# Low parts of the sixth token operand made by GpSimd instead of VectorE at three phase changes

## What is computed

```python
h = rmsnorm(x, norm_g)
proj = jnp.einsum('btd,dc->btc', h, w_in)
xa, za, v, bg, cg, zb, ga, gb = jnp.split(proj, SPLIT_IDX, axis=-1)
ya, new_pool = pool_mixer(xa, pool_buf, offset, w_pool_mix, pool_scale)
ya = ya * jax.nn.silu(za)
yc, new_conv = conv_mixer(cg * v, conv_buf, w_conv)
yb = bg * yc * jax.nn.silu(zb)
merged = (jax.nn.sigmoid(ga + b_gate[:D_MODEL]) * jnp.einsum('bte,ed->btd', ya, w_proj_pool)
          + jax.nn.sigmoid(gb + b_gate[D_MODEL:]) * jnp.einsum('bte,ed->btd', yb, w_proj_conv))
x = x + jnp.einsum('btd,de->bte', merged, w_out)
```

## Time and profile before

| | us |
|---|---|
| median of 3 runs | 2438.61 |
| lowest and highest run | 2438.40 and 2442.47 |
| the profiled execution | 2441.29 |
| its span, first to last instruction | 2439.3 |
| PE busy | 2400.9 (98%) |
| DVE busy | 1681.2 (69%) |
| ACT busy | 891.8 (37%) |
| GpSimd busy | 113.3 (5%) |

### The profile page before, as it was taken

How to read it: one execution, slowest core, us unless ns; L and a number is a source line. 1 busy time by engine, 2 the same in 40 slices (tenths; PEclk the granted TensorE clock), 3 DMA queues, 4 the chain that set the end, 5 groups by cost and what they waited for, 6 DMA issues and landing times.

```text
span 2439.3 us, 42617 instructions
## 1 busy us (share of the span) xinstructions
PE 2400.9 (98%) x17834; PEld 2338.0 (96%) x17834; DVE 1681.2 (69%) x2298; ACT 891.8 (37%) x1306; POOL 113.3 (5%) x216
## 2 busy tenths in 40 slices
PE   7999999999999999999999999999999999999997
PEld 6999999999999999999999999999999999888886
DVE  6556666666666686777868777865755876877666
ACT  7423333333333343323322222233533533432535
POOL 2000000000000000000000000000000011100001
PEclk9999999999999999999999999999999999999999
DMA  6454333333333453434433343245555767998656
GB/s 228 154 202 151 126 108 107 108 108 108 108 108 108 160 206 136 161 135 148 150 131 114 134 139 139 100 178 197 209 164 181 274 241 272 317 338 310 234 210 224
DMA packets 197069, 422.23 MB, mean 173 GB/s; under 512 B 12329, under 2 KB 113757, under 8 KB 182032
## 3 DMA queue, kind: packets, MB, share of 16 engines
q1 hardware_dynamic: 171200, 286.16, 34.6%
q0 software_dynamic: 24224, 127.33, 13.9%
q10 hardware_dynamic: 1456, 6.03, 0.7%
HBM read 283.10 MB, written 135.86 MB: 172 GB/s over the span
## 4 chain that ended last, share of the span: by engine, by line
PE 92%; DMA 3%; DVE 2%; ACT 1%; issue 1%; POOL 0%; ACTq 0%; SPq 0%; DVEq 0%
PE ps L1275 73%; PE ps L1400 10%; PE ps L1317 6%; PE ps L1462 1%; PE ps L1422 1%; DMA rest<-in_x_sample_dram 1%; DVE ops L2060 1%; DMA mt_raw<-opq 1%; DMA xn<-in_x_prompt_dram 1%; DMA tb_in<-opq 0%; DMA ops_raw<-opq 0%; DVE lo L1916 0%; ACT junk L1800 0%; PE ps L1438 0%; DVE pb L2055 0%
## 5 line engine op out<-in xcount | busy, mean ns | idle before, releaser
L1275 PE MATMUL ps<-ops,hi 128*128 128x272 f32 x9888 | 1349.1, 289 | 4.9 <-DVE pb L2055 4.0
L1275 PEld LDWEIGHTS ps<-ops,hi 128*128 128x128 f32 x9888 | 1286.3, 188 | 6.4 <-DVE pb L2055 4.7
L1275 PE MATMUL ps<-ops,lo 128*128 128x272 f32 x4944 | 720.6, 288 | 0.0
L1275 PEld LDWEIGHTS ps<-ops,lo 128*128 128x128 f32 x4944 | 658.4, 188 | 0.0
L1523 ACT ACTIVATE hi<-sb 128x512 fp32r<-128x512 f32 x432 | 273.2, 632 | 576.9 <-PE ps L1275 447.2
L2055 DVE TENSOR_TENSOR pb<-pb,ps 128x544 f32<-128x544 f32 x342 | 246.1, 720 | 268.0 <-PE ps L1275 267.8
L1916 DVE TENSOR_TENSOR lo<-sb,hi 128x512 fp32r<-128x512 f32 x432 | 297.6, 689 | 162.3 <-ACT hi L1523 158.3
L1523 ACT ACTIVATE hi<-raw 128x512 fp32r<-128x512 f32 x268 | 169.4, 632 | 371.2 <-PE ps L1275 358.6
L1916 DVE TENSOR_TENSOR lo<-raw,hi 128x512 fp32r<-128x512 f32 x268 | 184.7, 689 | 116.2 <-ACT hi L1523 116.2
L1400 PE MATMUL ps<-ms_hi,mt 128*128 128x512 f32 x896 | 222.7, 391 | 2.6 <-DVE mt L2298 2.6
L1400 PEld LDWEIGHTS ps<-ms_hi,mt 128*128 128x128 f32 x896 | 168.8, 189 | 38.6 <-DVE mt L2298 3.0
(11 more groups left out here) (158 smaller groups left out, 1510.9 us busy)
## 6 DMA issues: line engine op xcount, KB each, us to landing
raw<-in_w_in_dram SPq DMA_DIRECT2D x158, 512.0 KB, 3.9
pb<-part SPq DMA_DIRECT2D x39, 1088.0 KB, 6.1
part<-pb POOLq DMA_DIRECT2D x37, 1088.0 KB, 5.3
mt_raw<-opq SPq DMA_DIRECT2D x28, 1024.0 KB, 6.0
gates<-pb POOLq DMA_DIRECT2D x16, 1088.0 KB, 9.3
gate<-gates SPq DMA_DIRECT2D x32, 544.0 KB, 6.5
ms<-in_w_out_dram SPq DMA_DIRECT2D x16, 1024.0 KB, 9.8
ops_raw<-opq SPq DMA_DIRECT2D x15, 1088.0 KB, 6.9
```

The lines of the kernel that those rows point to most:

```text
L1275: mm = nc.tensor.matmul(ps[b][:, c, 0:HC], w[:, w_slot, kt * P:(kt + 1) * P], operand[:, kt, half, c * HC:(c + 1) * HC], start=fresh and k ...
```

## The change

GpSimd takes over the low part of operand 5, the sixth, at each of the three phase changes. `operand_lo` of DVE returns at once for it, and GpSimd has a function of its own with the same subtraction on the same tiles. It counts on a semaphore of its own, `pool_lo`, for which PE waits ahead of the second eight matmuls of q = 5. The counts of `ops_lo` become six per phase instead of seven (`lows_of`), at every place that waits for them.

```diff
+    BY_POOL = 5
+
+    def lows_of(ph, o):
+
+        return (NQ - 1) * (ph - 1) + o + (o < BY_POOL)
...
+        pool_lo = sem("pool_lo")
...
-                        sp.wait_ge(ops_lo, operands_of(YA, 6))
+                        sp.wait_ge(ops_lo, lows_of(YA, 6))
...
+            def operand_lo(ph, o):
+
+                pool.wait_ge(ops_hi, operands_of(ph, o))
+                nc.gpsimd.tensor_tensor(ops[:, o, :, 1, :], ops_raw[o][:, :, 1, :], f32(ops[:, o, :, 0, :]),
+                                        ALU.subtract).then_inc(pool_lo, 1)
...
+                if s in SPLIT and SPLIT[s][1] == BY_POOL:
+                    operand_lo(*SPLIT[s])
...
-                    halves = (ops_hi, ops_lo, operands_of(ph, q))
+                    halves = (ops_hi, ops_lo, operands_of(ph, q), lows_of(ph, q))
+                    if q == BY_POOL:
+                        halves = (ops_hi, pool_lo, operands_of(ph, q), ph)
...
             def operand_lo(ph, o):
+                if o == BY_POOL:
+                    return
                 dve.wait_ge(ops_hi, operands_of(ph, o))
```

More of the change, by code:

```diff
@@ L872, in load_operand @@
                     if ph == YB and o == 0:
-                        sp.wait_ge(ops_lo, operands_of(YA, 6))
+                        sp.wait_ge(ops_lo, lows_of(YA, 6))
                     if o == 6:
-                        sp.wait_ge(ops_lo, operands_of(ph, 0))
+                        sp.wait_ge(ops_lo, lows_of(ph, 0))
                     dst = waiting[ph][o][:, :, :]
@@ L1271, in terms @@
                     if w is hi and halves is not None:
-                        pe.wait_ge((halves[0], halves[1])[half], halves[2])
+                        pe.wait_ge(halves[half], halves[2 + half])
                     for kt in range(KQ):
@@ L1292, in first_product @@
                 place, _ = FIRST_OPS[f]
-                terms(i % 2, (SLOT0 + 4 * g + n) % R, ops[:, place], 4 * g + n + 1, (first_hi, first_lo, f + 1),
+                terms(i % 2, (SLOT0 + 4 * g + n) % R, ops[:, place], 4 * g + n + 1, (first_hi, first_lo, f + 1, f + 1),
                       i in (0, 1, 4, 5))
@@ L1360, in product @@
                 if g == NC:
-                    halves = (first_hi, first_lo, (1, 5, 6, 4, 7, 2, 8)[q])
+                    halves = (first_hi, first_lo, *2 * ((1, 5, 6, 4, 7, 2, 8)[q],))
                 elif ph > H0 and j == 0:
-                    halves = (ops_hi, ops_lo, operands_of(ph, q))
+                    halves = (ops_hi, ops_lo, operands_of(ph, q), lows_of(ph, q))
+                    if q == BY_POOL:
+                        halves = (ops_hi, pool_lo, operands_of(ph, q), ph)
                 terms(bank(s), s % R, ops[:, q], split_of_slot(s), halves, q in (0, 1, 5))
@@ L2099, in block_sums @@
                         dve.wait_ge(merged, 2 * ((ph - M0) * KQ + kt) + 2)
-                        dve.wait_ge(ops_lo, operands_of(YB, 6))
+                        dve.wait_ge(ops_lo, lows_of(YB, 6))
                 for k, (d, one, other) in enumerate(((dst[:, 0, :], src[1], src[0]),
@@ L2125, in window @@
                     else:
-                        dve.wait_ge(ops_lo, operands_of(H1, 6))
+                        dve.wait_ge(ops_lo, lows_of(H1, 6))
                 if c == 1 and k == 0:
```

## The result

| kernel | median, us | against before, 95% interval | profiled execution, us | its span, us |
|---|---|---|---|---|
| before | 2438.70 (6 runs) | | 2441.29 | 2439.3 |
| after | 2447.59 (6 runs, 2445.11 to 2448.83) | 1.0032 [1.0022, 1.0042] | 2447.26 | 2445.2 |

The changed kernel is slower: by 8.9 us between the medians, by 7.7 us (0.32%, to which the interval belongs) between the means. The whole interval lies beyond 0.2%. The six times of before form two groups, four at 2438.4 to 2438.8 us and two at 2441.7 and 2442.5 us, so that their median is uncertain by a microsecond; against the 33 further executions of before with which e1 to e4 are compared (median 2439.6) the changed kernel is 8.0 us slower. All executions compared in this document were in the fast state, but for one of e2 (2586.7 us at a granted clock of 0.849), which is left out of its ratio.

The account below looks back on a forecast made before the run. PE was taken to bound the kernel, with waits at three phase changes. From 2438.6 us, 6.8 us of moves and 3.0 of clock, 9.8 together, gave 2448.4 us; range 2434.3 to 2453, the forecast's own 2442.5 to 2453.

Parts of the forecast that it names:

- The bound: Whole kernel: PE, busy 2400.9 of 2439.3 us, bounds it; a microsecond PE stands still is one of the whole.
- What comes off DVE: At the three phase changes: three subtractions of 128x2176 leave DVE, 2.33 us each to the next step's start.
- GpSimd's time: Each moved subtraction on GpSimd, called D: 4.8 us, between 3.84 (two passes) and 5.8 (three passes).
- The mutual block: At the phase changes: while GpSimd reads SBUF, DVE steps with two SBUF inputs stand, as GpSimd does for them.
- The moves of q6: Delay of the new phase's seventh product (first pair, q0 to q6): 1.85, 2.5 and 2.45 us, 6.8 in all.
- The clock: Idle ahead of q6 at first and third change exceeds 1.97 us, so the clock falls: 1.5 us each, 3.0 together.
- Nothing is hidden: After the three changes: PE has no later mid-kernel wait to take up the loss, so all 9.8 us count.
- The size: Whole kernel: 6.8 us of moves plus 3.0 of clock, 9.8 us slower than before.
- The block that holds one way only: Rival at the phase changes: GpSimd waits for DVE but DVE goes on; 4.2 us back, 2434.4 us; chance 0.14.
- A quick GpSimd: Rival at the phase changes: GpSimd's step takes 2.5 to 3 us, no change, 2438.6 to 2440 us; chance 0.08.
- The turning point: GpSimd's time per step from which the forecast decides: D = 2.5.
- GpSimd giving way to each DVE step: Rival at the phase changes: GpSimd's read yields to every two-input DVE step; about 13 us lost, 2452 us; chance 0.10.

Follow-up runs that it names:

- e1: Against the changed kernel: GpSimd fills the tile with zeros two and a half times instead of subtracting, so it reads nothing; 2436.72 us, 0.9984 of before.
- e4: Against the changed kernel: GpSimd makes half of operand 5's low part, DVE the other half in the old place; 2444.08 us, 1.0014 of before.
- e2: Against the changed kernel: no engine makes operand 5's low part, PE reads the high part again; 2436.64 us, 0.9985 of before.
- e3: Against the changed kernel: GpSimd makes the low part of operand 1 instead of operand 5; 2442.61 us, 1.0010 of before.
- e8: Against the changed kernel: GpSimd copies operand 5's raw tile, one input read, instead of subtracting; 2436.94 us, 0.9992 of before.
- e7: Against the changed kernel: DVE drains q4 and makes operand 6's low part ahead of the weights' low part and sum; 2443.66 us, 1.0017 of before.

## Why the prediction was right, and where its sum was not

**The bound** stands: what holds PE up at the three places is what the change cost. That PE is busy for the same 2400.9 us in both kernels is chance, since a low clock counts as busy time: before, it fell at the second change (1.5 us) and at the join of the later phases (1.5 us), after, at the third change (2.6 us).

**What comes off DVE**, 3 x 2.33 us, is right; e2 has it alone, and DVE is busy for 7.1 us less there.

**GpSimd's time** was put at 4.8 us between 3.84 and 5.8. It is 4.88 us undisturbed (e3) and 4.75 us behind the end of DVE's step (all three changes). (The Trainium skill, GPSIMD Engine Reference, section Performance versus the Vector engine, has the figure from which the estimate of 4.8 us was worked out; e3's trace agrees with 4.88 us.)

**The mutual block** was taken from rows that showed one direction only the earlier trace rows. e1, e4 and e8 show the other. The moves of q6, term by term:

| change | predicted, us | measured, us |
|---|---|---|
| H0 to H1 | 1.85 | 2.36 - 0.63 = 1.73 |
| H1 to YA | 2.5 | 4.40 - 2.04 = 2.36 |
| YA to YB | 2.45 | 3.70 - 0.84 = 2.86 |
| sum | 6.8 | 6.95 |

At the third change 0.5 us are not from the block. Rows of ACT and DVE, the first from before, the others from after:

```profile
1925.75 2.42 DVE L2060 TENSOR_TENSOR ops<-ops_raw,ops 128x2176 fp32r<-128x2176 f32 x1
...
1923.61 0.62 ACT L1586 COPY pb<-ps 128x544 f32<-128x544 f32 x1 [2.50 <-DMA part_a<-pb]
...
1924.98 2.02 ACT L1592 CAST ops<-ops_raw 128x2176 fp32r<-128x2176 f32 x1 [0.23 <-DMA ops_raw<-opq]
...
1928.68 2.42 DVE L2079 TENSOR_TENSOR ops<-ops_raw,ops 128x2176 fp32r<-128x2176 f32 x1
```

Operand 4's low part, at whose end GpSimd gets in, started 6.37 us ahead of q5 before (1925.75 to 1932.12) and 5.86 us after (1928.68 to 1934.54): ACT had stood for a store, was late with a copy and then with the high part of operand 4. ACT's later wait of 0.58 us for operand 5 cost nothing, since that high part was there at 1930.64 and GpSimd could not begin before 1931.10. At the second change, PE did wait 0.99 us for GpSimd, and as predicted this added nothing to q6.

**The clock** is the term that was mis-sized. I added 1.5 us each at the first and third change and kept the 1.53 us of the second: 3.0 us. Measured: nothing at the first after 2.28 us without a weight load, the fall at the second gone after 3.30 us (-1.53), and at the third 5.38 - 3.01 = 2.4 us for q6 and 0.2 us more for the product behind it, after 3.29 us. In sum +1.1 us. The step that failed is "both over the 1.97 us behind which the clock fell at the second": longer than an idle that was followed by a fall does not mean a fall. e3 has the plainest pair, both in one execution: full level for q6 after 2.15 us at the second change, 0.62 after 2.16 us at the third.

**"Nothing is hidden"** failed in the profiled pair. The moves and the clock make 8.0 us, and the spans differ by 5.9. The difference is at the join of the later phases, where PE waits for DVE's `mt`. The prediction's "PE has no later wait in the middle of the kernel that would take it up" overlooked a row among the waits of PE in the trace of before:

```profile
PE ps L1400 <- DVE mt L2298: 2.6, 1, 2.6
```

It lies at 2114.6 us, behind all three changes, with a fall of the clock behind it that costs about 1.5 us; after, the wait is 1.7 us and the clock holds. Over the ten profiles this wait is 0.4 to 1.7 us in the four kernels that are slower than before (e7, e4, e3 and after) and 1.1 to 2.6 us in before and the five others. That looks as if a part of what is lost at the changes were made up there; with one execution of each it isn't shown.

**The size.** The median rose by 8.9 us where 9.8 were predicted, and part of this closeness is luck. The profiled execution of before (2441.29) is among the longest of its kernel and that of after (2447.26) is in the middle of its own, which is why the spans differ by less than the medians. By the means the change cost 7.7 us, by the larger number of runs of before 8.0. So the sum was too high by 1 to 2 us, which the clock term, 1.9 us too large, is enough to explain. How the time divides over moves and clock in the mean of many executions stays open, since the clock fell at different places in different profiles.

**The rivals.** The block that holds one way only would have given 2434.4 us and a DVE step of 0.69 us; DVE's step of 0.69 us is what e1 looks like, though its time is 2 us higher, and it isn't what the change does. A quick GpSimd was ruled out by its 4.88 us; e4 (2.4 us of reading, but with half of the step left on DVE) and e8 (1.87 us, time below before) show that this rival was a real one: the loss goes with GpSimd's time. The turning point itself, put at D = 2.5, no run has. GpSimd giving way to each DVE step did not happen: it was let in at the first gap each time and then kept the way to its end.

## What to carry to other kernels

Before an elementwise step is moved from DVE to GpSimd, look at what DVE does in the same microseconds: here, where its steps have two inputs in SBUF, it stood for as long as GpSimd read. What counted was then not how full the engines are but the time saved on DVE against GpSimd's time for the step, 2.33 against 4.8 us at each of three places. In the trace look for the longest instance of a group and not its mean: three steps of 4.75, 5.38 and 4.69 us among 268 of 0.69 us started the whole loss, and no idle time is shown for them.

## What the runs showed of the hardware

- GpSimd's subtraction of 128x2176 in fp32 takes 4.88 us, DVE's 2.42 us; GpSimd's copy of as much 1.87 us behind the end of DVE's step (4.75 us for the subtraction, counted likewise), its memset 1.92 us. A second input costs GpSimd 2.9 us and a first one next to nothing, which I had not expected from an estimate of even passes.
- The same DVE step of 128x512 took 0.69 us beside a GpSimd that writes, up to 2.49 us beside one that reads one input, and up to 5.40 us (e7) beside one that reads two. A DVE step with an input in PSUM kept its 0.71 us beside it.
- The granted clock of TensorE did not follow from the length of the idle ahead of it in these traces: at full level after 2.15 (e3), 2.28 and 3.30 us without a weight load, at 0.50 after 3.29 us, at 0.62 after 1.97 and 2.16 us (the latter in e3). A fall cost between 1.5 and 2.6 us.
